# A fused two-mixer encoder block on one core: weight sums of the up projections built in DRAM by accumulating transfers, and another order of sum, bank copy and operand split where the up projections begin

## The reference, cut to what matters

```python
h = x @ w_in + b_in                    # x: 1024 x 1024; w_in: 1024 x 5376
q_a,k_a,v_a,gate_a, q_b,k_b,v_b,gate_b, mg_a,mg_b = split(h)
o_a = sliding_window_attention(rope(q_a), rope(k_a), v_a, sinks) * silu(gate_a)
o_b = stick_breaking_attention(q_b, k_b, v_b) * silu(gate_b)
y_a = o_a @ w_up_a                     # 512 -> 1024, the up projections
y_b = o_b @ w_up_b                     # 512 -> 1024
sub = (sigmoid(mg_a) * y_a + sigmoid(mg_b) * y_b) @ w_out
out = layer_norm(alpha * x + sub) * ln_g + ln_b
```

## Time and profile before

| what | before |
|---|---|
| median of 3 executions | 721.74 us (721.46 to 722.67) |
| the profiled execution, its time | 722.17 us |
| its span, first to last instruction | 720.4 us |
| around the span | 1.8 us |
| PE busy | 707.2 us (98%), 3998 matmuls |
| DVE busy | 561.4 us (78%) |
| ACT busy | 446.7 us (62%) |
| POOL busy | 103.7 us (14%) |
| transfers | 77.27 MB, mean 107 GB/s |

### The profile page before, as it was taken

One profiled execution on the slowest core, in us unless ns is written; L12 is line 12 of the kernel. 1 busy time (PEld: TensorE's weight loads), 2 busy tenths in 40 slices (PEclk: granted clock), 3 DMA queues, 4 the chain that ended last, 5 costly groups with the idle time before them and its releaser, 6 DMA issues.

```text
span 720.4 us, 10882 instructions
## 1 busy us (share of the span) xinstructions
PE 707.2 (98%) x3998; PEld 577.8 (80%) x3998; DVE 561.4 (78%) x782; ACT 446.7 (62%) x776; POOL 103.7 (14%) x130
## 2 busy tenths in 40 slices
PE   8999999999999999999999999999998999999996
PEld 6888877777888888788888888888887888888885
DVE  6999788765987987898889784557779999990644
ACT  6954477776867767777686764565577655750421
POOL 0000000000322232132222310000000000000882
PEclk9999999999999999999999999999999999999999
DMA  8235332231100101020113214666324555830451
GB/s 297 113 90 126 107 94 84 74 98 43 50 31 30 60 30 59 3 88 16 45 30 117 74 45 144 219 233 208 117 82 153 170 166 159 310 118 1 160 190 58
DMA packets 44916, 77.27 MB, mean 107 GB/s; under 512 B 12352, under 2 KB 16960, under 8 KB 44864
## 3 DMA queue, kind: packets, MB, share of 16 engines
q1 hardware_dynamic: 44864, 76.59, 33.0%
HBM read 55.60 MB, written 18.87 MB: 103 GB/s over the span
## 4 chain that ended last, share of the span: by engine, by line
PE 96%; DVE 2%; DMA 1%; issue 1%; ACT 0%; SPq 0%; POOL 0%; POOLq 0%; DVEq 0%; ACTq 0%
PE ps L209 26%; PE ps L211 26%; PE ps L210 26%; PE ps L1789 5%; PE ps L1801 5%; PE ps L1774 4%; PE ps L1718 1%; PE ps L1730 1%; PE ps L1699 1%; DMA xr<-in_xt 1%; DVE keep L1455 1%; PE ps L1753 0%; PE ps L1687 0%; DVE o_t L1594 0%; DVE o_t L1585 0%
## 5 line engine op out<-in xcount | busy, mean ns | idle before, releaser
L209 PE MATMUL ps<-x_hi,w_hi 128*128 128x512 f32 x416 | 167.2, 402 | 1.9 <-DVE x_lo L1362 1.9
L211 PE MATMUL ps<-x_hi,w_lo 128*128 128x512 f32 x416 | 162.5, 391 | 0.0
L210 PE MATMUL ps<-x_lo,w_hi 128*128 128x512 f32 x416 | 162.2, 390 | 0.0
L1254 DVE TENSOR_TENSOR w_lo<-raw,w_hi 128x512 fp32r<-128x512 f32 x144 | 97.8, 694 | 47.9 <-ACT w_hi L772 47.4
L209 PE MATMUL ps<-t_ops,w_hi 128*128 128x512 f32 x288 | 115.8, 402 | 2.3 <-issue 2.3
L211 PE MATMUL ps<-t_ops,w_lo 128*128 128x512 f32 x288 | 113.2, 393 | 0.0
L210 PE MATMUL ps<-t_ops,w_hi 128*128 128x512 f32 x288 | 112.9, 392 | 0.0
L1455 DVE TENSOR_TENSOR_SCAN keep<-keep 128x895 f32<-128x895 f32 (+4 forms) x64 | 85.9, 1373 | 15.4 <-POOL keep L729 15.4
L209 PEld LDWEIGHTS ps<-x_hi,w_hi 128*128 128x128 f32 x416 | 78.2, 188 | 17.9 <-issue 3.4
L211 PEld LDWEIGHTS ps<-x_hi,w_lo 128*128 128x128 f32 x416 | 78.1, 188 | 16.8
L210 PEld LDWEIGHTS ps<-x_lo,w_hi 128*128 128x128 f32 x416 | 78.3, 188 | 14.6
(11 more groups left out here) (196 smaller groups left out, 1182.2 us busy)
## 6 DMA issues: line engine op xcount, KB each, us to landing
raw<-in_w SPq DMA_DIRECT2D x50, 256.0 KB, 2.9
raw<-in_w SPq DMA_DIRECT2D x24, 512.0 KB, 3.8
sig_m<-sig_d SPq DMA_DIRECT2D x16, 512.0 KB, 4.7
sig_d<-sig_m SPq DMA_DIRECT2D x28, 256.0 KB, 2.7
xr<-in_xt SPq DMA_DIRECT2D x16, 256.0 KB, 6.1
o_t<-o_d SPq DMA_DIRECT2D x8, 512.0 KB, 4.9
raw<-in_xn SPq DMA_DIRECT2D x8, 512.0 KB, 3.7
out<-o_t SPq DMA_DIRECT2D x16, 256.0 KB, 2.2
```

The lines of the kernel that those rows point to most:

```text
L209: pe.matmul(out, w_hi, x_hi, start=first, stop=False, skip_group_check=goes_on)
L210: pe.matmul(out, w_hi, x_lo, start=False, stop=False, skip_group_check=goes_on)
L211: return pe.matmul(out, w_lo, x_hi, start=False, stop=last, skip_group_check=goes_on)
L1254: dve.tensor_tensor(ring_slot(w_lo, q), part_of(q), ring_slot(w_hi, q).bitcast(F32), ALU.subtract).then_inc(part_lo, 1)
```

## The change

The four weight sums of the four up pairs no longer come from DVE. At the start of the program POOL issues eight transfers of 1 MB from DRAM to DRAM, four of them plain copies and four that add to what is there (`accum_op`), in five stages with a wait between them; they leave the operands 5, 6, 7 and 3 in `up_sum_d`. For the up products SP then loads one 256 KB operand per product (`load_up`) into five places in turn, five products ahead of its rounding, where it had loaded 1 MB per pair. To suit an accumulation that can only add, some sums change sign (`up_sums`, the bank copies of positions 4 and 6 with scale -1, one `add_block` that subtracts).

The order changes where the up projections begin. `next_parts` gives one product per step from product 138 on. On DVE the last sum of the input projection (`add_block(19, 2)`) moves from after product 138 into the split of position 3, between its two instructions. On ACT the split of position 4 moves from the end of `after(139)` to `after(140)`, behind the read of product 140's bank.

```diff
 def next_parts(q):
-    return {0: (q + 3, q + 4), 5: (), 6: (q + 3,)}.get(q % NP, (q + 4,)) if q < ALL_PRODUCTS - 4 else ()
+    if q >= LAST_PAIR + 5:
+        return (q + 4,) if q < ALL_PRODUCTS - 4 else ()
+    return {0: (q + 3, q + 4), 5: (), 6: (q + 3,)}.get(q % NP, (q + 4,))
+def up_raw_loads(q):
+    if q < LAST_PAIR + 3:
+        return {LAST_PAIR: (N_PRODUCTS, N_PRODUCTS + 1), LAST_PAIR + 1: (N_PRODUCTS + 2, N_PRODUCTS + 3),
+                LAST_PAIR + 2: (N_PRODUCTS + 4,)}.get(q, ())
+    return (q + 4 + UP_RAWS,) if q + 4 + UP_RAWS < ALL_PRODUCTS else ()
...
+            def load_up(q):
+                n = q - N_PRODUCTS
+                if n < UP_RAWS:
+                    sp.wait_ge(part_lo, LAST_PAIR + (4, 5, 3, 6, 7)[n])
+                else:
+                    sp.wait_ge(part_lo, q - UP_RAWS + 1)
+                if n == 2:
+                    sp.wait_ge(w_sum, 4 * N_PAIRS)
+                    sp.wait_ge(up_summed, 16 * 8)
...
+                sp.dma_start(up_raw(q), src).then_inc(up_in[n % UP_RAWS], 16)
...
+            pool.wait_ge(x_lo_done, 2 * KT)
+            pool.dma_start(up_sum_d[5], up_quarter(1, 0)).then_inc(up_summed, 16)
+            pool.dma_start(up_sum_d[7], up_quarter(0, 0)).then_inc(up_summed, 16)
+            pool.dma_start(up_sum_d[3], up_quarter(0, 1)).then_inc(up_summed, 16)
+            pool.wait_ge(up_summed, 16 * 3)
+            pool.dma_start(up_sum_d[5], up_quarter(1, 1), accum_op=ALU.add).then_inc(up_summed, 16)
+            pool.dma_start(up_sum_d[7], up_quarter(1, 0), accum_op=ALU.add).then_inc(up_summed, 16)
+            pool.wait_ge(up_summed, 16 * 5)
+            pool.dma_start(up_sum_d[6], up_sum_d[5]).then_inc(up_summed, 16)
+            pool.wait_ge(up_summed, 16 * 6)
+            pool.dma_start(up_sum_d[6], up_quarter(0, 0), accum_op=ALU.add).then_inc(up_summed, 16)
+            pool.wait_ge(up_summed, 16 * 7)
+            pool.dma_start(up_sum_d[3], up_sum_d[6], accum_op=ALU.add, max_dma_last_dim=4 * HALF).then_inc(up_summed, 16)
             for s in range(STEPS):
                 cut_causal(s)
...
+                if q == N_PRODUCTS:
+                    for ab in range(2):
+                        branch_hi(UP_SPLITS[q - 1], ab)
                 for n in next_parts(q):
                     part_high(n)
-                if q in UP_SPLITS:
+                if q in UP_SPLITS and q != N_PRODUCTS - 1:
                     for ab in range(2):
                         branch_hi(UP_SPLITS[q], ab)
...
                     if q in UP_SPLITS:
                         branch_lo(UP_SPLITS[q], ab)
+                    if (q, ab) == (LAST_PAIR + 4, 0):
+                        add_block(N_PAIRS - 1, 2)
...
-                if pos in (4, 5) and i + 1 < ALL_PAIRS:
+                    if (i, k) != (N_PAIRS - 1, 2):
+                        add_block(i, k)
+                if pos in (4, 5) and i + 1 < N_PAIRS:
                     weight_sums(i + 1, pos == 4)
```

More of the change, by code:

```diff
@@ L167, in next_parts @@
 def next_parts(q):
-    return {0: (q + 3, q + 4), 5: (), 6: (q + 3,)}.get(q % NP, (q + 4,)) if q < ALL_PRODUCTS - 4 else ()
+    if q >= LAST_PAIR + 5:
+        return (q + 4,) if q < ALL_PRODUCTS - 4 else ()
+    return {0: (q + 3, q + 4), 5: (), 6: (q + 3,)}.get(q % NP, (q + 4,))
+UP_RAWS = 5
+def up_raw_loads(q):
[3 more added lines that the diff above has]
+    return (q + 4 + UP_RAWS,) if q + 4 + UP_RAWS < ALL_PRODUCTS else ()
 def ring_order():
@@ L315, in build @@
         sig_d = nc.dram_tensor("sig_d", (KT, 2, P, SEQ), F32, kind="Internal").ap()
+        up_sum_d = {n: nc.dram_tensor(f"up_sum{n}_d", (P, UP_PAIRS, HALF), F32, kind="Internal").ap()
+                    for n in (5, 6, 7, 3)}
         gate_d = nc.dram_tensor("gate_d", (GROUP, P, SEQ), F32, kind="Internal").ap()
@@ L418, in ring_slot, with up_raw, up_quarter @@
             return t[:, q // 2 % 2, half(q % 2)]
+        def up_raw(q):
+            n = (q - N_PRODUCTS) % UP_RAWS
+            return (raw[:, 1, half(0)], raw[:, 0, half(0)], w_x[:], raw[:, 0, half(1)], raw[:, 1, half(1)])[n]
+        up_tiles = w[UP_0:UP_0 + KT].rearrange("(j m) p c -> m p j c", m=2)
+        def up_quarter(m, kh):
+            return up_tiles[m][:, :, half(kh)]
         def part_of(q):
+            if q >= N_PRODUCTS:
+                return up_raw(q)
             which = ORDER[q % NP]
@@ L456, in build, with up_arrived @@
         a11_in, a12_in, a2_in = sem("a11_in"), sem("a12_in"), sem("a2_in")
+        up_in = (a2_in, a11_in, raw_in[0], a12_in, raw_in[1])
+        up_summed = sem("up_summed")
         const_in = sem("const_in")
+        def up_arrived(n):
+            return up_in[n % UP_RAWS], 16 * (n // UP_RAWS + 1 + (1 if n % UP_RAWS in (2, 4) else N_PAIRS))
         first_in = [[sem(f"first_in{n}_{i}") for i in range(2)] for n in range(2)]
@@ L530, in load_a2 @@
                 sp.dma_start(raw[:, 1, :], w[tile_of(i, 1)]).then_inc(a2_in, 16)
+            def load_up(q):
[7 more added lines that the diff above has]
+                    sp.wait_ge(up_summed, 16 * 8)
+                j, which = n // NP, ORDER[n % NP]
+                if which in up_sum_d:
+                    src = up_sum_d[which][:, j, :]
+                else:
+                    src = w[UP_0 + 2 * j + (which == 4)][:, half(which != 1)]
+                sp.dma_start(up_raw(q), src).then_inc(up_in[n % UP_RAWS], 16)
             def swap_halves(i, b):
@@ L623, in after @@
                         up_gates(j, 2)
-                if pos < 2 and i + 1 < ALL_PAIRS:
+                if pos < 2 and i + 1 < N_PAIRS:
                     load_a1(i + 1, pos)
-                if pos == 2 and i + 1 < ALL_PAIRS:
+                if pos == 2 and i + 1 < N_PAIRS:
                     load_a2(i + 1)
+                for n in up_raw_loads(q):
+                    load_up(n)
                 if i in Q_PAIRS and pos in (2, 4, 5, 6):
@@ L759, in part_high @@
                 i, which = q // NP, ORDER[q % NP]
-                if which == 1:
+                if i >= N_PAIRS:
+                    act.wait_ge(*up_arrived(q - N_PRODUCTS))
+                elif which == 1:
                     act.wait_ge(a11_in, 16 * (i + 1))
@@ L882, in read_bank @@
                     act.activation(up_other(pos) if pos % 2 else up_made(b), ps[:, 2 * (q % 2):2 * (q % 2) + 2, :],
-                                   ACT.Copy).then_inc(bank_read, 1)
+                                   ACT.Copy, scale=-1.0 if pos in (4, 6) else 1.0).then_inc(bank_read, 1)
                 elif pos % 2:
@@ L1230, in add_block @@
                     o = up_made((0, 2, 1)[k])
-                    dve.tensor_tensor(o, o, up_other(2 * k + 1), ALU.add).then_inc(block_sum, 1)
+                    dve.tensor_tensor(o, o, up_other(2 * k + 1),
+                                      ALU.subtract if k == 1 else ALU.add).then_inc(block_sum, 1)
                     return
@@ L1283, in up_sums @@
                             dve.wait_ge(o_back[k], 16)
-                    dve.tensor_tensor(o, quarter_of(0, 1), quarter_of(0, 0), ALU.subtract).then_inc(u_raw[t], 1)
+                    dve.tensor_tensor(o, quarter_of(0, 0), quarter_of(0, 1), ALU.subtract).then_inc(u_raw[t], 1)
                 elif t == 2:
@@ L1287, in up_sums @@
                     dve.wait_ge(z_done, STEPS)
-                    dve.tensor_tensor(o, quarter_of(1, 1), up_sum(1, ab), ALU.subtract).then_inc(u_raw[t], 1)
+                    dve.scalar_tensor_tensor(out=o, in0=up_sum(1, ab), scalar=-1.0, in1=quarter_of(1, 1), op0=ALU.mult,
+                                             op1=ALU.subtract).then_inc(u_raw[t], 1)
                 elif t == 3:
@@ L1294, in up_sums @@
                     dve.wait_ge(ol_done, 2 + ab + 1)
-                    dve.tensor_tensor(o, o, up_sum(2, ab), ALU.subtract).then_inc(u_raw[t], 1)
+                    dve.scalar_tensor_tensor(out=o, in0=up_sum(2, ab), scalar=-1.0, in1=o, op0=ALU.mult,
+                                             op1=ALU.subtract).then_inc(u_raw[t], 1)
             def branch_lo(pos, ab):
@@ L1348, in sums @@
                 for k in {1: (0,), 4: (1,), 5: (2,)}.get(pos, ()):
-                    add_block(i, k)
-                if pos in (4, 5) and i + 1 < ALL_PAIRS:
+                    if (i, k) != (N_PAIRS - 1, 2):
+                        add_block(i, k)
+                if pos in (4, 5) and i + 1 < N_PAIRS:
                     weight_sums(i + 1, pos == 4)
```

## The result

The changed kernel took 724.91 us (median of 6, 724.12 to 726.64); the kernel before, timed beside it, 722.12 (median of 6). The ratio is 1.0045, with a 95% interval of 1.0034 to 1.0055: slower by 2.8 us, where 2.9 us less was forecast. The profiled execution took 725.54 us with a span of 723.8, which is 3.4 us longer than before.

What follows compares the result with a forecast made beforehand. PE, at work for 98% of the span, was taken as the bound. -3.95 + 1.06 = -2.89 us took the profiled 722.17 to 719.28; with the median 0.43 lower, the forecast was 718.9 us, range 717.6 to 720.8.

Steps and rivals of the forecast that it cites:

- What the chain disturbs: SP's pair 1 load issued at 38.08, beside POOL's transfers: 0.7 to 1.4 us late, inside 2.15 us of cover, cost 0.
- Slower, by that same load: Rival, chance 0.05: pair 1's load 6.0 us late behind POOL's backlog, PE waits 3.85 plus 1.73 at low clock, 724.4 us.
- DVE at 543 to 549: Before the up projections, DVE's third sum starts at 545.88 instead of 548.36.
- ACT at 545 to 549: ACT reads product 140's bank from 548.38, so PE's wait at 142 and its clock drop go: -3.95 us.
- What is late next: ACT's read of 141, behind four splits, ends at 554.59, so PE has a new wait of 1.06 us at product 143.
- The second wait and the clock: The wait at product 143 doesn't lower PE's clock; rival, chance 0.12: it does, costing 1.73 us, 720.6 us.
- Loads of the up weights: SP's 28 loads of 256 KB replace 12, each about 2.8 us with 13.6 us of cover: cost 0.
- The eight transfers: POOL's transfers start at 20.7 us and end between 53 and 75, with over 100 us of cover before step 0.

Runs made afterwards that it cites:

- the late chain: Changed kernel, but POOL begins its eight transfers only after the rope work (at 96.2 us) instead of after the low parts of x: 719.71 us, ratio 0.9976.
- the run with the small pieces: Changed kernel with the plain copy of sum 5 to sum 6 in pieces of 2 KB instead of 64 KB: 724.67 us, ratio 1.0039.
- the chain alone: Kernel before with POOL's eight transfers added at 20.8 us, their result read by nobody: 732.95 us, ratio 1.016.
- the chain of plain copies: Changed kernel with its four additions made plain copies in pieces of 2 to 4 KB, so the sums are lost: 719.37 us, ratio 0.9971.
- the order-only kernel: Kernel before with only the new order of sums and splits on DVE and ACT, weight sums left on DVE: 720.15 us, ratio 0.9988.

## Why the prediction was wrong

**The step that failed** is "What the chain disturbs", with its "I take 0". It failed in two ways.

First, the size. The delay was put at 0.7 to 1.4 us, "if the chain takes turns with it". The part of the delay in which the two queues take turns was 1.4 us, so that estimate held. What it leaves out, a term put at nothing without a word, are the 2.4 us in which no packet of the load moved at all. Together they are 3.85 us against a cover of 2.15; the difference, 1.7, is near the 1.45 us that PE lost at product 6. Without the adding the load was 1.8 us late and the cover held; the wait for the first packet is not the adding's alone, since the late chain's plain copies made one as long.

What I made of the Trainium skill (DMA: Bandwidth & Descriptors, "Queues, rings and completion order") was too kind. The trace agrees that the load is not put behind the whole backlog: it landed at 44.47, and the transfer of the chain issued at 34.10 was waited for until 51.00. I had read the rule as turns of one profile packet each, and once both queues move, the trace bears this out (127 and 126 packets, one for one). But the same sentence of the page says that an engine drains a whole packet, typically 9 to 17 descriptors, before it goes to another queue. The 2.4 us ahead of the load's first packet, some 15 chain packets of the profile on each engine, are of that size; that they were one such turn is not shown, and the turns that follow are not like it. What holds the first packet back stays open.

Second, the scope. I looked at one load, the one with the least cover on ACT, and not at the other transfers in 40 to 80 us. Of the sixteen 64 KB transfers of attention operands, the last six, issued from 59.26 on, took 6.6 us and more instead of about 2. SP's stream stood at one issue for 4.61 us, beside the copy, and pair 2's loads were issued 6.0 us late and took 5.6 us. The larger of the two waits, 3.22 us and 1.69 at the low clock, comes from there, and by the run with the small pieces it is the addition, more than the hold at the copy, that sets when the load lands. Those transfers are in no row that I had read.

**The rival "Slower, by that same load"** gave 724.4, and 724.9 was measured. It was the mechanism in kind: a weight load late beside the chain, PE waiting 3 to 4 us, and the low clock behind it. That the number came so near is luck: its sum was one wait of 3.85, where there were two of 1.45 and 3.22. It got 0.05 because it was tied to a condition ("if queues don't take turns") that the trace shows only ahead of a first packet.

**DVE at 543 to 549, ACT at 545 to 549: right.** Product 142 starts without a wait. The last matmul of product 140 starts at 551.58 + 11 x 0.227 = 554.08 and the read of its bank at 554.50, 0.42 later, where about 0.4 was forecast.

**What is late next: right.** Product 143 was due at 559.74 and started at 560.84: 1.10 us, where 1.06 was forecast, behind the same read of 141.

**The second wait and the clock: right here.** The granted clock was 1.00 from 559 to 564 us.

**Loads of the up weights: right.** From product 144 on, PE is on its beat.

**The eight transfers: the end was a little late.** It came at 78.9 against 53 to 75: an accumulating 1 MB, one at a time, took 9.9 and 10.4 us, and two together, issued at 33.45 and 34.10, were waited for until 51.00: above the upper end of 8.1 us each. It costs nothing on POOL: the cover of more than 100 us was there.

**What stays open.** Why nothing of a load moves for up to 3.4 us when it meets a busy queue. For the chain alone against the whole change, the traces show the meeting that decided: one transfer of SP, issued 0.95 us ahead of an addition in the one and 0.68 us behind it in the other. That the scatter of the early waits from one execution to the next (1.29 and 3.05; 1.22, 2.46 and 0.65) comes from such meetings is argued.

## What to carry to other kernels

A bulk transfer on a queue of its own is not free because its own result is needed late: list every transfer of the other queues in the stretch where it runs, with its cover, and follow the streams that stand behind them. Put it where loads have cover to spare; here one more wait on POOL turned a ratio of 1.0045 into 0.9968. Cost a bulk transfer of 1 MB at several microseconds for each load beside it, plain or adding; one that adds as it writes took up to twice as long as a copy (two together 16.6 us against 8.0), so it meets more of them.

## What the hardware showed that was not expected

- The packets of the accumulating transfers held an engine for 181 ns each (337 of them, 2 KB each on average); while POOL's plain copies ran, 22 to 28 us in the changed kernel, 445 packets of 4 KB on average took 75.4% of 16 engines' 6 us, 163 ns. Per byte the addition costs 2.2 times the copy.
- A load of 256 KB took 2.7 to 3.4 us in the kernel before, 4.3 to 7.9 beside accumulations, 3.2 to 6.3 beside the chain of plain copies, and 8.7 and 9.1 beside three plain copies issued together.
- Two queues that both moved passed packets one for one: 127 packets of 2 KB and 126 of 256 bytes in the same 1.5 us. So a transfer in small packets gets the smaller share of the bytes: 64 KB of them took 6.6 to 8.9 us instead of 2.2, part of it ahead of the first packet.
- Waits of like length are followed by the low clock in one execution and not in another: 3.05 us in the changed kernel (0.66 behind it) and 2.46 in its repetition (1.00 from 71 to 76 us); 1.93 in the order-only kernel (0.66) and 2.41 in the chain-only kernel (1.00 from 65 to 75). The length of the wait alone does not tell, so a term for it belongs into the range.
